# Attention steps over two key heads: 64-row score matmuls, 64-column value matmuls, one softmax per step

## What is computed

```python
def nsa_core(q, q_rot, qpos, ck, cv, fetch, wk, wv, wpos, gates, key_len):
    ...
    s = jnp.einsum('bqghd,bgqkd->bghqk', q_rot, k_sel).astype(jnp.float32) * SCALE
    smask = (kpos <= qpos[None, None, :, None])[:, :, None]
    p_slc = jax.nn.softmax(jnp.where(smask, s, NEG_INF), axis=-1)
    o_slc = jnp.einsum('bghqk,bgqkd->bqghd', p_slc.astype(v_sel.dtype), v_sel)
    s = jnp.einsum('bqghd,bwgd->bghqw', q_rot, wk).astype(jnp.float32) * SCALE
    ...
    p_win = jax.nn.softmax(jnp.where(wmask, s, NEG_INF), axis=-1)
    o_win = jnp.einsum('bghqw,bwgd->bqghd', p_win.astype(wv.dtype), wv)
    o = gates[..., 0:1] * o_cmp + gates[..., 1:2] * o_slc + gates[..., 2:3] * o_win
```

## Time and profile before

| | |
|---|---|
| median of 3 runs | 1514.22 us (1513.03 to 1515.32) |
| the profiled execution's own span | 1521.6 us |
| PE busy, whole span | 1469.1 us (97%) |
| PEld, DVE, ACT, POOL busy | 1322.9, 577.0, 484.7, 515.6 us |
| mean granted clock of PE | 0.980 |
| scores (line 974), 256 records | 86.0 us |
| values (line 1020), 160 records | 81.0 us |
| transposes of P (line 1008), 320 records | 53.2 us |
| `row_max` (line 1260), 128 records | 60.7 us |

### The profile page before, as it was taken

The page is one execution under the profiler, slowest core; times in us unless marked ns, Lnnn a source line. Parts: engine busy times, 40 slices in busy tenths (PEclk is TensorE's granted clock), DMA queues, the critical chain, the costliest instruction groups (busy, mean ns, idle before and its releaser), DMA issues.

```text
span 1521.6 us, 26668 instructions
## 1 busy us (share of the span) xinstructions
PE 1469.1 (97%) x10754; PEld 1322.9 (87%) x10754; DVE 577.0 (38%) x985; ACT 484.7 (32%) x731; POOL 515.6 (34%) x136
## 2 busy tenths in 40 slices
PE   7997999999999999999898999999899999999998
PEld 6997999999999999999584445447799999999997
DVE  5347442222223333143556555552242222223232
ACT  5311342232232333112015556552233222223232
POOL 6422334334336555332201000000233443444652
PEclk9998999999999999999979999999899999999999
DMA  5221222332322333353610000006233223222332
GB/s 188 84 84 56 85 84 83 101 92 83 94 82 77 95 95 111 111 133 120 125 54 22 1 1 1 0 1 184 46 100 95 83 84 109 83 74 82 89 95 76
DMA packets 208062, 124.02 MB, mean 82 GB/s; under 512 B 30964, under 2 KB 205100, under 8 KB 207998
## 3 DMA queue, kind: packets, MB, share of 16 engines
q1 hardware_dynamic: 207998, 123.14, 27.6%
HBM read 117.75 MB, written 5.38 MB: 81 GB/s over the span
## 4 chain that ended last, share of the span: by engine, by line
PE 50%; issue 33%; POOL 10%; SPq 2%; DMA 2%; DVE 1%; ACT 1%; POOLq 0%; DVEq 0%; ACTq 0%
PE PG L430 31%; POOL WL L1632 10%; PE PG L974 5%; PE M L1020 5%; PE M L1008 3%; PE M L947 2%; DMA WBD<-in_w_cmp 1%; PE PG L958 1%; POOL SQX L1627 1%; DMA SLOT<-in_cache_win 1%; PE M L1120 1%; SPq L785 1%; PE M L908 1%; SPq L789 1%; SPq L790 0%
## 5 line engine op out<-in xcount | busy, mean ns | idle before, releaser
L1632 POOL TENSOR_TENSOR WL<-WR,WH 128x2048 fp32r<-128x2048 f32 x105 | 484.6, 4615 | 691.4 <-ACT WH L490 691.4
L430 PE MATMUL PG<-H,WH 128*128 128x260 f32 x4128 | 671.4, 285 | 18.7 <-DVE P L1855 11.0
L430 PEld LDWEIGHTS PG<-H,WH 128*128 128x128 f32 x4128 | 568.4, 190 | 21.3 <-DVE P L1855 11.4
L430 PE MATMUL PG<-H,WL 128*128 128x260 f32 x2064 | 417.5, 283 | 0.0
L430 PEld LDWEIGHTS PG<-H,WL 128*128 128x128 f32 x2064 | 319.7, 189 | 0.0
L430 PE MATMUL PG<-G,WH 128*128 128x260 f32 x1920 | 309.2, 283 | 1.5 <-DVE G L1392 1.5
L490 ACT ACTIVATE WH<-WR 128x2048 fp32r<-128x2048 f32 x105 | 200.4, 1908 | 275.5 <-PE PG L430 243.6
L430 PEld LDWEIGHTS PG<-G,WH 128*128 128x128 f32 x1920 | 263.7, 189 | 1.7 <-issue 1.7
L430 PE MATMUL PG<-G,WL 128*128 128x260 f32 x960 | 194.0, 283 | 0.0
L430 PEld LDWEIGHTS PG<-G,WL 128*128 128x128 f32 x960 | 148.5, 189 | 0.0
L607 DVE TENSOR_TENSOR TB<-PG,RSTD 128x520 f32<-128x520 f32 x44 | 30.8, 699 | 213.0 <-PE PG L430 213.0
(11 more groups left out here) (228 smaller groups left out, 1071.0 us busy)
## 6 DMA issues: line engine op xcount, KB each, us to landing
WR<-in_w_ffn_in SPq DMA_DIRECT2D x88, 512.0 KB, 4.6
WR<-in_w_in SPq DMA_DIRECT2D x32, 512.0 KB, 4.4
WR<-in_w_ffn_out SPq DMA_DIRECT2D x32, 384.0 KB, 3.8
WR<-in_w_ffn_out SPq DMA_DIRECT2D x32, 320.0 KB, 3.2
WR<-in_w_in SPq DMA_DIRECT2D x18, 256.0 KB, 3.5
WR<-in_w_out SPq DMA_DIRECT2D x8, 512.0 KB, 3.8
PST<-in_cache_kv SPq DMA_DIRECT2D x32, 128.0 KB, 2.1
WR<-in_w_out SPq DMA_DIRECT2D x16, 256.0 KB, 5.9
```

The costliest lines, as they stand in the source:

```text
L430: mm = pe.matmul(PG[:, par, hf, 0:HALF], w, x, start=(first and at_k == 0 and n == 0), stop=(last and at_k == nk - 1 and n == 2))
L1632: w_split.on(pool.tensor_tensor(WL[:, b, :], WR[:, b, :], WH[:, b, :].bitcast(F32), ALU.subtract))
```

## The change

A step is now a pair jp of query tiles and a branch, over both key heads of the pair gp: still four heads, now two of each key head. `KP` holds both key heads one above the other with no zeros, so POOL clears two blocks less, and DVE writes it with four instructions in place of eight. The score matmul of a head has 64 rows, in the upper or the lower half of the array; the two of a query tile follow each other, into banks of their own, and the four masks come behind all four. The value matmul of a key tile becomes two of 64 stationary columns and 256 moving columns, into the upper and the lower half of `M`. `s_done`, `nb_ok` and `p_ready` count steps, no longer heads: one reduction over four heads, four exponentials, one reciprocal of four sums, one small product with four gates, and one `tensor_tensor` over all four heads with the factors broadcast. The waits on `at_g` count two less.

```diff
--- before.py
+++ after.py
@@ 
...
         WBD = at("WBD", [P, 2, 32, P], F32, wh_at)
-        (QR, KP), e = packed(h_at, ("QR", [P, KD, T], F32), ("KP", [P, 2, NKV, SEQ], F32))
+        (QR, KP), e = packed(h_at, ("QR", [P, KD, T], F32), ("KP", [P, 2, 2, SEQ], F32))
         assert e <= g_at
@@ 
...
         PAIRS = [(gp, i) for gp in range(2) for i in range(QT)]
-        STEPS = [(gp, i, e, br) for gp, i in PAIRS for e in range(2) for br in range(2)]
+        STEPS = [(gp, i, jp, br) for gp, i in PAIRS for jp in range(2) for br in range(2)]
@@ 
...
             clear(WBD[HD:P, :, :, 0:HD])
-            clear(KP[0:HD, :, 1:NKV:2, :])
-            clear(KP[HD:P, :, 0:NKV:2, :])
             pool.wait_ge(cmp_done.sem, 2)
...
             pool.wait_ge(w_split.sem, 2 + S0["out1"] + 1)
-            pool.wait_ge(s_done.sem, 4 * len(STEPS))
+            pool.wait_ge(s_done.sem, len(STEPS))
             pool.wait_ge(qs_ok.sem, 1)
@@ 
...
             def scores(hu):
-                gp, i, e, br = STEPS[hu]
+                gp, i, jp, br = STEPS[hu]
                 n = (i + 1) * P
...
                     pe.wait_ge(kp_ok.sem, 1)
-                    pe.wait_ge(at_g.sem, 8)
-                for j in range(4):
+                for jj in range(2):
                     if hu:
-                        pe.wait_ge(exp_done.sem, 4 * (hu - 1) + j + 1)
-                    bank = PG[:, j // 2, j % 2, :]
-                    pe.matmul(bank[:, 0:n], QR[:, gp * 4 + j, i * P:(i + 1) * P], KP[:, br, 2 * gp + e, 0:n],
-                              start=True, stop=False)
-
-                    s_done.on(pe.matmul(bank[:, n - P:n], CBF[:, 0:P], CBF[:, P:2 * P], start=False, stop=True))
+                        pe.wait_ge(exp_done.sem, 4 * (hu - 1) + 2 * jj + 2)
+                    for e in range(2):
+                        r = slice(e * HD, (e + 1) * HD)
+                        pe.matmul(PG[:, jj, e, 0:n], QR[r, gp * 4 + 2 * jp + jj, i * P:(i + 1) * P], KP[r, br, gp, 0:n],
+                                  start=True, stop=False)
+                for jj in range(2):
+                    for e in range(2):
+                        mm = pe.matmul(PG[:, jj, e, n - P:n], CBF[:, 0:P], CBF[:, P:2 * P], start=False, stop=True)
+                s_done.on(mm)
@@ 
...
-                gp, i, e, br = STEPS[hu]
+                i = STEPS[hu][1]
                 return [(q_pair[hu // 4], None)] * (hu % 4 == 0) + [(q_step[hu] + kt, kt) for kt in range(i + 1)]
...
-                gp, i, e, br = STEPS[hu]
+                gp, i, jp, br = STEPS[hu]
                 bank = q_bank(pe, q)
...
                     pe.wait_ge(c_ready.sem, gp + 1)
+                else:
+                    pe.wait_ge(p_ready.sem, hu + 1)
                 for j in range(4):
-                    if kt is not None:
-                        pe.wait_ge(p_ready.sem, 4 * hu + j + 1)
                     if kt is None:
...
                     else:
-                        mm = pe.transpose(bank[:, j * P:(j + 1) * P], PB[:, hu % 2, j, kt * P:(kt + 1) * P], IDENT)
+                        e, jj = j // 2, j % 2
+                        mm = pe.transpose(bank[:, j * P:(j + 1) * P], PB[:, hu % 2, 2 * jj + e, kt * P:(kt + 1) * P], IDENT)
                 q_fill.on(mm)
...
             def pv(hu, q, kt):
-                gp, i, e, br = STEPS[hu]
+                gp, i, jp, br = STEPS[hu]
                 q_wait_drained(pe, q)
...
                 else:
-                    r = slice(e * HD, (e + 1) * HD)
-                    c = gp * P + e * HD
-                    pv_done.on(pe.matmul(M[r, 2 + hu // 4 % 2, :], VTK[:, kt, br, c:c + HD], PT[:, (q - Q_ATT) % 4, :],
-                                         start=False, stop=br == 1 and kt == i))
+                    for e in range(2):
+                        c = gp * P + e * HD
+                        mm = pe.matmul(M[e * HD:(e + 1) * HD, 2 + hu // 4 % 2, 2 * jp * P:2 * (jp + 1) * P],
+                                       VTK[:, kt, br, c:c + HD], PT[:, (q - Q_ATT) % 4, 2 * e * P:2 * (e + 1) * P],
+                                       start=False, stop=jp == 1 and br == 1 and kt == i)
+                    pv_done.on(mm)
@@ 
...
             for gp in range(2):
-                for e in range(2):
-                    r = slice(e * HD, (e + 1) * HD)
-                    for br in range(2):
-                        c = dve.tensor_scalar(KP[r, br, 2 * gp + e, :], P0[r, KV_TILE[br] + gp, 0:SEQ], SCALE, None, ALU.mult)
+                for br in range(2):
+                    c = dve.tensor_scalar(KP[:, br, gp, :], P0[:, KV_TILE[br] + gp, 0:SEQ], SCALE, None, ALU.mult)
             kp_ok.on(c)
@@ 
...
-                gp, i, e, br = STEPS[hu]
+                i = STEPS[hu][1]
                 o = 4 * (hu % 2)
-                for j in range(4):
-                    dve.wait_ge(s_done.sem, 4 * hu + j + 1)
-                    nb_ok.on(dve.tensor_reduce(NB[:, o + j:o + j + 1], PG[:, j // 2, j % 2, 0:(i + 1) * P], AX.X, ALU.max,
-                                               negate=True))
+                dve.wait_ge(s_done.sem, hu + 1)
+                nb_ok.on(dve.tensor_reduce(NB[:, o:o + 4], PG[:, :, :, 0:(i + 1) * P].rearrange("p a b k -> p (a b) k"),
+                                           AX.X, ALU.max, negate=True))
...
-                gp, i, e, br = STEPS[hu]
+                gp, i, jp, br = STEPS[hu]
                 o = 4 * (hu % 2)
-                for n in range(5):
-                    if n < 4:
-                        dve.wait_ge(exp_done.sem, 4 * hu + n + 1)
-                        vec.on(dve.reciprocal(F[:, o + n:o + n + 1], SUM[:, o + n:o + n + 1]))
-                    if n:
-                        j = n - 1
-                        pj = PB[:, hu % 2, j, 0:(i + 1) * P]
-                        g = 3 * (4 * (2 * gp + e) + j) + 1 + br
-                        dve.wait_ge(vec.sem, vec.now - (n < 4))
-                        p_ready.on(dve.tensor_scalar(pj, pj, F[:, o + j:o + j + 1], GT[:, i, g:g + 1], ALU.mult, ALU.mult))
+                gate = GT[:, i, :].rearrange("p (g e a b x) -> p g a b e x", g=2, e=2, a=2, b=2, x=3)[:, gp, jp, :, :, 1 + br]
+                f = F[:, o:o + 4]
+                pj = PB[:, hu % 2, :, 0:(i + 1) * P]
+                dve.wait_ge(exp_done.sem, 4 * hu + 4)
+                chain(dve.reciprocal(f, SUM[:, o:o + 4]))
+                chain(dve.tensor_tensor(f.rearrange("p (b e) -> p b e", b=2), f.rearrange("p (b e) -> p b e", b=2), gate,
+                                        ALU.mult))
+                p_ready.on(dve.tensor_tensor(pj, pj, f.unsqueeze(2).to_broadcast([P, 4, (i + 1) * P]), ALU.mult))
@@ 
...
                 r, tiles, row0 = split_heads(gp, e)
-                dve.wait_ge(at_g.sem, 10)
+                dve.wait_ge(at_g.sem, 8)
                 for rot, src in ((0, QS[r, tiles, :]), (1, QU[r, tiles, :])):
@@ 
...
             copies.append((PTN[0:NS, n, :], src[0:NS, 2 * P:3 * P]))
-            drains(eng, mine, q, copies, [(at_g.sem, 10 + n)])
+            drains(eng, mine, q, copies, [(at_g.sem, 8 + n)])
@@ 
...
             def exps(hu):
-                gp, i, e, br = STEPS[hu]
-                o, n = 4 * (hu % 2), (i + 1) * P
+                o, n = 4 * (hu % 2), (STEPS[hu][1] + 1) * P
                 if hu >= 2:
...
                 for j in range(4):
-                    act.wait_ge(nb_ok.sem, 4 * hu + j + 1)
+                    if j == 0:
+                        act.wait_ge(nb_ok.sem, hu + 1)
                     exp_done.on(act.activation(PB[:, hu % 2, j, 0:n], PG[:, j // 2, j % 2, 0:n], ACT.Exp,
...
                                                accum_out=SUM[:, o + j:o + j + 1]))
```

## The result

| | before | after |
|---|---|---|
| time, median of four (range) | 1514.72 us (1513.03 to 1515.32) | 1608.04 us (1602.75 to 1612.35) |
| ratio, 95% interval | | 1.0595 (1.0563 to 1.0626) |
| span of the profiled execution | 1521.6 us | 1610.5 us |
| attention phase, first transposes to sample group | 805.26 to 1028.90: 223.6 us | 808.28 to 1121.95: 313.7 us |
| its 31 turns by 128 / 256 / 384 / 512 keys | 32.5 / 44.6 / 60.5 / 79.2 us | 43.1 / 68.2 / 91.6 / 103.4 us |

What follows compares the result with a forecast made beforehand. TensorE's two matmul kinds bound the kernel before. Ring 55 plus clock 34 make 89 us on the profiled 1521.6, so 1610.6; median 7.4 lower, 1603 us. The forecast's own range was 1580 to 1625, the overall range 1553 to 1645.

Steps and rivals of the forecast that it cites:

- the last step of the sum: From profiled span to measured time: the median lies 7.4 us below the span, so 1610.6 becomes 1603 us.
- The loop: Attention phase: each step becomes a chain of waits through TensorE, VectorE and ScalarE, making the phase 55 us longer.
- the ring: One attention step's transposes, scores and four-head softmax in sequence: 5.3, 7.7, 9.8 and 11.8 us at 128 to 512 keys.
- The softmax pieces: Attention step without transposes and scores: 3.8, 5.3, 6.8 and 8.3 us at 128, 256, 384 and 512 keys.
- Scores side by side: Four heads' 64-row score matmuls partly overlap, taking five units of time, bounded by four and eight: 2.6 us at 512 keys.
- S: Time of a step's score matmuls up to the last mask's start: 2.6 us at 512 keys, 2.05, 1.5 and 1.0 below.
- The clock: Attention phase: TensorE's holes lower its clock, costing 1.1 us a step, 34 us over 31; bounds nothing and 82.
- The rival in which the clock stays up: Attention phase: the clock stays at its upper level; 1569 us, or 1561 with the best scores; chance 0.17.
- the one in which it stays low: Attention phase: the clock stays low from step to step, 55 + 82 us more, 1651 us; chance 0.13.
- The covers costed at nothing: Keys' copy and two cleared GpSimd blocks less: no gain, since VectorE idles 13.70 us behind the copy; otherwise 1.5 us.
- The stall beside GpSimd: One softmax instruction ran 3.44 us beside GpSimd's weight split; it may go, and was left out of the sum.
- The faster rival: Attention phase: TensorE still paces the steps, 8.0 us at 512 keys, phase 45 us shorter, 1469 us; chance 0.05.

Runs made afterwards that it cites:

- the experiment that does this part alone: The kernel before with its own matmuls, only the softmax of a step made one chain for four heads: 1623.86 us, ratio 1.0687.
- the waits filled: The kernel after with five f32 matmuls that nobody reads added in each step where TensorE otherwise waits: 1577.52 us, ratio 1.0391.

## Why the prediction was right, and where it was off

The forecast was 1603 us with the phase 89 us longer; it was 1608.0 and 90.0. The 5 us between the times are the last step of the sum: it took the median 7.4 us below the profiled span, as in the kernel before, and in the kernel after it lies 2.5 below. The span itself, 1610.5 against 1610.6, is nearer than the terms deserve, as the errors below show. By its steps:

**The loop.** Right: the ring as it was laid out is the chain of waits of the kernel after, piece by piece, and the experiment that does this part alone (+111 us) shows that the chain is the cause and the narrow matmuls are not. By keys the sum had 37.1, 61.6, 78.4 and 94.4 us of turns; with the waits filled they are 41.0, 59.4, 81.6 and 92.4.

**The softmax pieces.** From the start of the reduction to the end of the scaling the timeline has 3.42, 4.92, 6.41 and 7.90 us at 128 to 512 keys. With the 0.14 to the transposes and the 0.26 ahead, as the prediction counted, that is 3.8, 5.3, 6.8 and 8.3, its four numbers. A per-instruction cost plus a per-element cost (155 ns and 1.044 ns) from two shapes of the kernel before carried to an instruction four times as long, and to a reduction over four banks.

**Scores side by side.** Mis-sized, on the safe side. From the first score matmul to the reduction I had S + 0.26: 1.26, 1.76 and 2.86 us at 128, 256 and 512 keys; at the upper clock it was 1.09, 1.50 and 2.36 to 2.42. The five units that I took were four: the matmuls of the two heads start 0.01 us apart, and the next two 0.43 behind them, so the start order of a head's two instructions costs nothing here. Over 31 rings, transposes and scores at the upper clock come to 80.2 us by the timeline (384 keys interpolated) where the sum had about 91, its extra for second tiles included.

**The clock.** Right in size, and now measured in two ways. Taking each turn's transposes and scores against their time at the upper clock gives 39.7 us (5.5, 8.9, 16.1 and 9.2 by keys), of which 0.8 isn't the clock but VectorE subtracting output rows ahead of one reduction, the 1 us of the sum; filling the waits shortens the phase by 33.4, with some of the loss still in it (and by 35.0 where the clock went to 1.00, on the matmuls of before). The term was 34. The 1.1 us a step that it is added up from was my estimate, and no run shows it as such; over the 31 turns the two measures come to 1.3 and 1.1 us a turn. The rival in which the clock stays up falls by the windows of 0.74 and 0.75; the one in which it stays low falls by steps such as that at 921.22, where the scores run at the upper one. One row that speaks for the lower clock behind the hole is weak: the four transposes of 1.27 us there follow the scaling head by head, and four that did the same took 1.19 at the upper clock; the lower clock there stands on the granted clock alone, 0.50 in the microsecond from 820 and 0.70 in that from 822.

**What the sum did not have.** 4.2 us in three turns: the transposes found TensorE still busy with values at the lower clock (after steps 14 and 30, 1.66 us each; after step 17, 0.8). And the last step's values took 6.6 us for an estimated 5. With the 11 too many for the scores the errors cancel: 177.7 for softmax, 4.5 hand-overs, 80.2, 39.7 and 4.2 make 306.3, with 0.8 ahead and 6.6 behind 313.7. The near hit in the total is in part this cancelling, which is luck. The ring's 55, against 56.6 with the waits filled, is no cleaner: there transposes and scores took 86.5 us, 4.5 less than the sum had, and late transposes of 4.6 us make that up.

**The covers costed at nothing.** The keys' copy was rightly put at nothing. It shrank from 3.07 us to 1.42, VectorE's wait behind it grew from 13.70 to 16.01, and the instruction behind that wait was released by TensorE in both kernels.

The stall beside GpSimd is another matter. The ring was summed without it because one broadcast tensor_tensor showed no stretching, but that row did not run beside the weight split. In the kernel after the split ran from 820.43 to 824.93 and the gate product started after it, at 825.13; a reduction beside it (822.60) took its usual 0.69 us. With the waits filled the same work comes sooner, and the gate product runs into the split:

```profile
812.91 4.52 POOL L1635 TENSOR_TENSOR WL<-WR,WH 128x2048 fp32r<-128x2048 f32 x1 [12.25 <-ACT WH L490]
...
816.43 1.02 DVE L1277 TENSOR_TENSOR ST<-ST,GT 128x4 f32<-128x4 f32 x1
```

It ends as the split ends, at 817.45 and 817.43, and takes 1.02 us where it takes 0.17 elsewhere. The same product took 2.40 us with the softmax by pairs, and 0.88 to 1.14 in three more of the kernels above, each time until the split ended. So the term came out at nothing in the kernel after because of when its gate product started, not because a tensor_tensor is spared.

**The side that lost.** The faster rival asked that the softmax fit under what TensorE has left after the scores. That fails with four heads in one instruction (8.3 us at 512 keys against 4.5), and the kernel with the softmax by heads shows what the same matmuls give when the softmax isn't one chain: 7.53 us a step. The prediction judged the change as given; it did not say that the packing with the softmax left by heads was worth 1.9%.

## What to carry to other kernels

Merging the softmax of several heads into one long instruction saves a fixed cost per instruction (155 ns here) on an engine that has time (VectorE, busy for 577.0 us of 1521.6), and makes each head wait for the last one at every hand-over; where a loop runs over engines with one set of buffers, add up the ring for the merged and for the split form before counting instructions. Here, work that was cut from TensorE had to be counted twice, once as time if it is on the path, and once as cover for the clock if it is not. When packing shortens matmuls, keep the hand-overs fine: pairs side by side with a softmax and a signal for each head gave the gain here (1492.85 us), the softmax by pairs gave none over the kernel before (1513.04), and the single chain turned it into a loss (1608.04).

## What the runs showed of the hardware

Two f32 matmuls on different 64-row halves, into different banks, run side by side: four heads of 512 keys took 1.92 us from the first score matmul to the first mask, against 3.43 over 128 rows, 1.8 times as long. In the trace the 128-row records start 0.43 us apart, at both ends of their group too; the 64-row ones start in twos, 0.01 us apart, with 0.43 us from one two to the next but 0.53 behind the first two and 0.52 from the last two to the mask. So they overlap fully among themselves, and each end of the group, where the tile shape changes, took another 0.1 us. I had expected a part of the overlap to be lost to the order of the two instructions that each f32 score matmul is (256 records and 256 weight loads for the 128 of the kernel before). S, up to the start of the last mask, came out at 2.10 us at 512 keys, where the prediction had 2.6, and 2.17 with four units.

The records of neighbours overlap: a 128-row score record of 512 keys lasts 0.59 us and the next one starts 0.43 behind its start. The lengths given here are therefore read from start to start.

Removing TensorE work that nobody waits for went with a slower kernel: 1623.86 us with wide values, 1637.40 with narrow ones, and with unread matmuls in the waits of both they are 1595.29 and 1589.76. Adding such matmuls took 29 to 48 us off three kernels; the granted clock over the phase went from 0.75 to 0.96, from 0.78 to 0.97 and from 0.86 to 1.00.

Behind most of the waits of 2.5 to 5 us in the kernel after, though not behind all, TensorE's next pieces ran at a lower granted clock: over the microsecond behind the wait it was 0.50 to 0.57 after 20 of 25, and 0.95 and 1.00 after two. Two transposed tiles took 1.87 us at 0.50, from their start to the first score matmul, instead of 0.99 to 1.02 at 1.00, and scores up to the reduction as much as 3.65 (the clock at 0.64 over them) instead of 2.4, within a ring in which the softmax pieces kept their durations (a reduction of 2.29 us in each 512-key turn).

A small tensor_tensor (2 or 4 elements in each partition) that started while GpSimd's weight split ran ended with the split, in five kernels, at 0.88 to 2.40 us instead of 0.16 or 0.17; reductions beside the split kept their durations (0.69 us over four heads of 128 keys).
